# Small linears with both weight parts in one tile, first chunks split by VectorE, row loads later, work reordered at ten places

## What is computed

```python
# block 1: latent attention, 16 heads
c_q, c_kv, k_rope, z = split(x @ w_in, [512, 1024, 1088])
q = rmsnorm(c_q) @ w_qb;  kv = rmsnorm(c_kv) @ w_kvb;  k_rope = rope(k_rope)   # k_rope: 64 columns
x = layernorm(ALPHA*x + (attn(q, k, v) * silu(z)) @ w_out)
# block 2: mLSTM, 8 heads; gates: 16 columns of w_in
qk, v, o, gates, z = split(x @ w_in);  qk = silu(conv4(qk))
x = layernorm(ALPHA*x + (sigmoid(o) * rmsnorm(cell(qk, v, gates)) * silu(z)) @ w_out)
# block 3: mod = silu(c) @ w_ada + b_ada -> sh1, sc1, g1, sh2, sc2, g2
h = rmsnorm(x) * (1 + sc1) + sh1
x += g1 * ((sigmoid(ga) * (attn_a(h) @ w_oa) + sigmoid(gb) * (attn_b(h) @ w_ob)) @ w_out)
h = rmsnorm(x) * (1 + sc2) + sh2
x += g2 * ((silu(h @ w_gate) * (h @ w_up)) @ w_down);  out = rmsnorm(x) * final_w
```

## Time and profile before

| | |
|---|---|
| median of 3 runs | 2233.73 us (2232.44 to 2234.04) |
| profiled execution: its time, its span | 2235.4 us, 2233.7 us |
| TensorE busy, in the span | 2194.4 us (98%) |
| VectorE, ScalarE, GpSimd busy | 1496.7, 1008.7, 265.5 us |
| mean granted TensorE clock | 0.995 of full speed |
| DMA | 500.72 MB, mean 224 GB/s |

### The profile page before, as it was taken

One profiled execution on the slowest core, in us unless ns is written; L12 is line 12 of the kernel. 1 busy time (PEld: TensorE's weight loads), 2 busy tenths in 40 slices (PEclk: granted clock), 3 DMA queues, 4 the chain that ended last, 5 costly groups with the idle time before them and its releaser, 6 DMA issues.

```text
span 2233.7 us, 32562 instructions
## 1 busy us (share of the span) xinstructions
PE 2194.4 (98%) x10958; PEld 1855.2 (83%) x10958; DVE 1496.7 (67%) x2004; ACT 1008.7 (45%) x1229; POOL 265.5 (12%) x499
## 2 busy tenths in 40 slices
PE   9999999999999998999999999999999999999997
PEld 7898878988887777899888888888888888888886
DVE  5766668877666878588776768775565655444544
ACT  5445544544444434434565444454444444443433
POOL 2101110112110010701101111110000100000000
PEclk9999999999999999999999999999999999999999
DMA  8877577679885585968756886766776776565563
GB/s 292 231 192 242 166 255 246 190 224 298 268 270 175 160 302 183 225 219 262 226 180 189 289 279 237 234 218 203 256 228 226 243 247 210 177 221 183 187 200 132
DMA packets 200428, 500.72 MB, mean 224 GB/s; under 512 B 31816, under 2 KB 59112, under 8 KB 200048
## 3 DMA queue, kind: packets, MB, share of 16 engines
q1 hardware_dynamic: 166544, 394.62, 55.1%
q0 software_dynamic: 33760, 104.41, 14.5%
HBM read 496.84 MB, written 2.15 MB: 223 GB/s over the span
## 4 chain that ended last, share of the span: by engine, by line
PE 88%; DVE 6%; ACT 2%; DMA 2%; issue 2%; SPq 0%; DVEq 0%; POOLq 0%; ACTq 0%; POOL 0%
PE ps L2085 74%; PE ps L2123 9%; DVE lo L1149 1%; DMA raw<-in_ml_w_in_dram 1%; ACT hi L660 1%; DVE acc_s L1161 1%; PE ps L2499 1%; PE ps L2489 1%; DMA ada_raw<-in_w_ada_dram 0%; PE ps L2150 0%; DVE conv_tmp L1583 0%; PE ps L2571 0%; PE ps L2161 0%; DMA raw<-in_ml_w_out_dram 0%; PE ps L2414 0%
## 5 line engine op out<-in xcount | busy, mean ns | idle before, releaser
L1149 DVE TENSOR_TENSOR lo<-raw,hi 128x1024 fp32r<-128x1024 f32 x731 | 890.3, 1223 | 573.9 <-ACT hi L660 570.6
L660 ACT CAST hi<-raw 128x1024 fp32r<-128x1024 f32 x731 | 763.2, 1051 | 999.4 <-PE ps L2085 789.0
L2085 PE MATMUL ps<-hi,XH 128*128 128x512 f32 x1944 | 613.4, 395 | 9.0 <-DVE lo L1149 4.7
L2085 PE MATMUL ps<-lo,XH 128*128 128x512 f32 x1944 | 603.3, 390 | 0.0
L2085 PE MATMUL ps<-hi,XL 128*128 128x512 f32 x1944 | 602.4, 390 | 0.0
L2085 PEld LDWEIGHTS ps<-hi,XL 128*128 128x128 f32 x1944 | 365.5, 188 | 77.5
L2085 PEld LDWEIGHTS ps<-lo,XH 128*128 128x128 f32 x1944 | 365.3, 188 | 77.2
L2085 PEld LDWEIGHTS ps<-hi,XH 128*128 128x128 f32 x1944 | 359.7, 188 | 83.4 <-DVE lo L1149 7.5
L578 POOL DMA_DIRECT2D ada_raw<-in_w_ada_dram x384 | 206.2, 537 | 1575.8 <-DVE acc_s L1161 933.1
L1161 DVE SCALAR_TENSOR_TENSOR acc_s<-ada_raw,c_act,acc_s 128x512 f32<-128x512 f32 x256 | 191.0, 746 | 11.7 <-DMA ada_raw<-in_w_ada_dram 10.6
L2123 PE MATMUL ps<-XH,hi 128*128 (+1 forms) x512 | 145.5, 284 | 0.2 <-DVE XL L1300 0.2
(11 more groups left out here) (357 smaller groups left out, 1840.7 us busy)
## 6 DMA issues: line engine op xcount, KB each, us to landing
ada_raw<-in_w_ada_dram POOLq DMA_DIRECT2D x384, 256.0 KB, 4.5
raw<-in_w_in_dram SPq DMA_DIRECT2D x136, 512.0 KB, 4.5
raw<-in_ml_w_in_dram SPq DMA_DIRECT2D x128, 512.0 KB, 4.6
raw<-in_w_gate_dram SPq DMA_DIRECT2D x176, 256.0 KB, 3.0
raw<-in_w_up_dram SPq DMA_DIRECT2D x176, 256.0 KB, 3.6
raw<-in_w_down_dram SPq DMA_DIRECT2D x88, 512.0 KB, 4.2
raw<-in_mla_w_in_dram SPq DMA_DIRECT2D x47, 512.0 KB, 4.5
raw<-in_mla_w_out_dram SPq DMA_DIRECT2D x32, 512.0 KB, 4.7
```

The lines of the kernel that those rows point to most:

```text
L660: nc.scalar.copy(hi[:, j, :], raw[:, j, :]).then_inc(hi_ready, 1)
L1149: nc.vector.tensor_tensor(lo[:, j, :], raw[:, j, :], hi[:, j, :].bitcast(F32), ALU.subtract) \
L2085: ins = mm(ps[:, o:o + HALF], x, w[:, b % RING, c0:c0 + HALF], start=first, stop=(k == n_rows - 1 and x is xl), skip_group_check=True)
```

## The change

It does the following.

- **Small linears:** `small_hi` and `small_lo` become one tile `small_parts`; per 128 rows one matmul of 256 columns takes both parts by XH (128 or 104 weight columns), a second takes the high part by XL. The two partial sums lie in different PSUM partitions. For `kr` they are added by the turn, which multiplies by a table `fold` (two identities on top of each other) instead of an identity; for `gates` VectorE adds them with two more instructions. GpSimd zeroes 1024 instead of 640 columns of `small_raw`, ScalarE casts as many.
- **First chunks:** of `cT` and of `yTa` VectorE makes the high parts of chunks 0 and 1 itself, each followed by its low part; ScalarE starts at chunk 2.
- **First blocks by token half:** the first block of `qr`, `mz1`, `lo0` and `wo0` starts with token half 0 as soon as the reader of that half is done (`first_free`); half 1 waits for the whole reader.
- **yTa** is turned in two halves, the first block of `lo0` between them; the last head's result for the second token half moves behind the first two splits.
- **mlq:** its first block runs all hi x XH, then hi x XL, then lo x XH (`feature_first`), and its `lo_block` stands after the first split.
- **MLA loop:** the second cast of a double slot moves behind `mla_lo` of the next k; ada sums go to the slots without casts (2 less the number of casts).
- **conv:** ScalarE's silu of `mlq` and `mlk` one block later.
- **Row loads** of `lo0` and `lo1`: at blocks 14, 17, 20 and 23 in place of 10, 12, 14 and 16, the tables behind them at 25, 26 and 28.
- **wo0 and ffn0:** the first split of `mTa` before the second product of `ob1`; `lo_block` of ffn0's block 0 before the last rms; both columns of `ada2` in one go before the turn; the second half of `normalise_second` after `modulation`.
- **Tail:** the product of X's first token half by `final_row` moves from VectorE (`last_rows(0)`) to GpSimd, its scaling to ScalarE.

```diff
-        small_hi = at("small_hi", 132, [P, KD, ROPE], F32R)
-        small_lo = at("small_lo", 136, [P, KD, ROPE], F32R)
+        small_parts = at("small_parts", 132, [P, KD, 2, ROPE], F32R)
...
-                if b == 10:
+                if b == 14:
                     sp.wait_ge(tile_split, SPLIT_BASE["yTb"] + 8)
-                if b in (10, 12):
-                    half_row("rows1", row_w, ln_w, 1, (b - 10) // 2)
-                if b in (14, 16):
-                    half_row("rows1", row_b, ln_b, 1, (b - 14) // 2)
-                if b == 18:
+                if b in (14, 17):
+                    half_row("rows1", row_w, ln_w, 1, (b - 14) // 3)
+                if b in (20, 23):
+                    half_row("rows1", row_b, ln_b, 1, (b - 20) // 3)
+                if b == 25:
                     load("window", window[:, :], cst("window"))
-                if b == 22:
+                if b == 26:
                     load("tables2", cos2[:, :, :].rearrange(flat), cst("cos"))
                     load("tables2", sin2[:, :, :].rearrange(flat), cst("sin"))
+                if b == 28:
...
+            pool.wait_ge(ev("final_row"), 16)
+            pool.wait_ge(ev("x_squares"), 9)
+            nc.gpsimd.tensor_tensor(X[:, 0, COLS:], X[:, 0, COLS:], final_row[:, COLS:], ALU.mult) \
+              .then_inc(ev("last_weighted"), 1)
...
-            def mla_casts(slot):
-                for b in MLA_CASTS[slot]:
+            def mla_casts(slot, n0=0, n1=1):
+                for b in MLA_CASTS[slot][n0:n1]:
...
+                if k >= 8:
+                    mla_casts(2 * k - 1 if k == 8 else k + 7, 1, 2)
...
+                    act.wait_ge(ev("last_weighted"), 1)
+                    nc.scalar.mul(X[:, 0, COLS:], X[:, 0, COLS:], ry[:, 0:1]).then_inc(ev("result2"), 1)
...
+                if k < 2:
+                    link(nc.vector.tensor_scalar(CH[:, k, :], ps[:, g + k * SEQ:g + (k + 1) * SEQ], col("q_norm", k),
+                                                 None, ALU.mult))
+                else:
+                    dve.wait_ge(ev("c_hi"), (k | 1) - 1)
                 nc.vector.scalar_tensor_tensor(out=CL[:, k, :], in0=ps[:, g + k * SEQ:g + (k + 1) * SEQ],
...
-            def mla_casts(slot):
-                for b in MLA_CASTS[slot]:
+            def mla_casts(slot, n0=0, n1=1):
+                for b in MLA_CASTS[slot][n0:n1]:
                     lo_block(B_Z0 + b, b % RING)
 
+            mla_sums = [0]
+
             def mla_ada(slot):
-                name, r = ("z0", "mo0")[slot // 16], slot % 16
-                for m in range(ADA_BESIDE[name] * r // 16, ADA_BESIDE[name] * (r + 1) // 16):
-                    ada_block((ADA_FIRST[name] + m) // KD, (ADA_FIRST[name] + m) % KD)
+                for _i in range(2 - len(MLA_CASTS[slot])):
+                    m = ADA_FIRST["z0"] + mla_sums[0]
+                    ada_block(m // KD, m % KD)
+                    mla_sums[0] += 1
 
             for k in range(24):
...
+                if k > 16:
+                    mla_casts(k + 7)
+                if k >= 8:
+                    mla_casts(2 * k - 1 if k == 8 else k + 7, 1, 2)
                 if k < 8:
-                    mla_casts(2 * k)
+                    mla_casts(2 * k, 0, 2)
                 if k < MLA_H:
                     mla_maximum(k)
                 slot = 2 * k + 1 if k < 8 else k + 8
                 if k < 8:
                     mla_ada(slot - 1)
-                mla_casts(slot)
+                if k < 16:
+                    mla_casts(slot)
                 mla_ada(slot)
+            mla_casts(31)
+            assert mla_sums[0] == ADA_BESIDE["z0"] + ADA_BESIDE["mo0"]
 
             def first_residual():
                 dve.wait_ge(ev("x"), 64)
...
-            split_y("yTa", 0, range(8))
+            dve.wait_ge(tiles_turned, BANKS_BEFORE["yTa"] + 1)
+            split_y("yTa", 0, range(2))
+            head_result(7, (1,))
+            split_y("yTa", 0, range(2, 8))
...
                             first3(n0)
+                            split_merged("mTa", 0)
...
+            lo_block(B_FFN, 0)
             rms_token(1, 6, None)
-            normalise_second(2)
-            lo_block(B_FFN, 0)
+            normalise_second((0,))
             modulation("ada2", "norm2", True)
+            normalise_second((1,))
             split_operand(0, "h2_full", B_FFN)
...
                         for tok in range(TOK):
+                            if first_free is not None and b == 0 and tok == 1:
+                                start(name)
                             ins = token_part(g, nb * per_block, H, L, b, tok, per_block, sub)
...
+            def feature_first(n0, g, H, L, need):
+
+                pe.wait_ge(hi_ready, n0 + 1)
+                pe.wait_ge(*need(0))
+                for w, x in ((hi, H), (hi, L), (lo, H)):
+                    if w is lo:
+                        pe.wait_ge(lo_ready, n0 + 1)
+                    for m in range(8):
+                        o = g + m * SEQ
+                        ins = mm(ps[:, o:o + SEQ], w[:, 0, m * P:(m + 1) * P], x[:, 0, :],
+                                 start=w is hi and x is H and m % 2 == 0, stop=False, skip_group_check=True)
+                ins.then_inc(block_done, 1)
+
+            def feature_major(name, n0, nb, H, L, need=None, blocks=None, hi_first=False):
...
                 for k in range(KD):
-                    for w, x in ((small_hi, XH), (small_hi, XL), (small_lo, XH)):
-                        ins = mm(ps[0:n, g:g + SEQ], w[:, k, 0:n], x[:, k, :],
-                                 start=(k == 0 and w is small_hi and x is XH),
-                                 stop=(k == KD - 1 and w is small_lo), skip_group_check=True)
+                    mm(ps[0:ROPE + n, g:g + SEQ], small_parts[:, k, :, :].rearrange(flat)[:, 0:ROPE + n], XH[:, k, :],
+                       start=k == 0, stop=False, skip_group_check=True)
+                    ins = mm(ps[0:n, g:g + SEQ], small_parts[:, k, 0, 0:n], XL[:, k, :], start=False,
+                             stop=k == KD - 1, skip_group_check=True)
                 done(ins)
...
             pe.wait_ge(M2["y"], 8)
-            transposes("yTa", operand_tiles(oz, 0), {8: (M2["h"], 15), 12: (M2["h"], 16)})
             y_tiles = lambda k: (tile_split, SPLIT_BASE["yTa"] + k + 1)
-            token_major("lo0", B_LO, 16, XH, XL, y_tiles, blocks=(0, 6))
+            transposes("yTa", operand_tiles(oz, 0)[:8])
+            token_major("lo0", B_LO, 16, XH, XL, y_tiles, blocks=(0, 1), first_free=(ev("mz1_first"), 1))
+            transposes("yTa", operand_tiles(oz, 0)[8:], {0: (M2["h"], 15), 4: (M2["h"], 16)})
+            token_major("lo0", B_LO, 16, XH, XL, y_tiles, blocks=(1, 6))
             pe.wait_ge(M2["y"], 16)
...
-            ada_columns("ada2", (0, 1), 20,
-                        lambda: (start("h2Ta"), turn_first("h2Ta", h_norm, h2_ready, first_token)))
-            turn_first("h2Ta", h_norm, h2_ready, second_token)
+            ada_columns("ada2", (0, 1), 20)
+            start("h2Ta")
+            turn_first("h2Ta", h_norm, h2_ready, [(k, t) for k in range(8) for t in range(TOK)])
```

More of the change, by code:

```diff
@@ L701, in each_tok @@
                         ins = nc.scalar.copy(dst(tok), src(T(name, tok, width)))
+                    if tok == 0 and first is not None:
+                        ins.then_inc(first, 1)
                 ins.then_inc(freed_sem["act"], 1)
@@ L790, in _ @@
             first3(B_QR)
-            each_tok("z1", lambda t: z_tok[:, t, COLS:], ACT.Silu)
+            each_tok("z1", lambda t: z_tok[:, t, COLS:], ACT.Silu, first=ev("z1_first"))
             g = grp("cT")
-            for k in range(8):
+            for k in range(2, 8):
                 if k % 2 == 0:
@@ L1752, in rms_token, with normalise_second @@
                 rsqrt(1, 1.0 / D, src, ev("rms"), at=tok)
-            def normalise_second(n):
-                for half in range(n):
+            def normalise_second(halves):
+                for half in halves:
                     cols_ = slice(half * COLS, (half + 1) * COLS)
@@ L2052, in _ @@
             last_quarter(0)
-            last_rows(0)
             last_quarter(1)
@@ L2367, in _ @@
             x1_tiles = chunks_ready("x1Ta")
-            feature_major("mlq", B_CONV, 16, XH, XL, x1_tiles, blocks=(0, 5))
+            feature_major("mlq", B_CONV, 16, XH, XL, x1_tiles, blocks=(0, 5), hi_first=True)
             pe.wait_ge(ev("normed0"), 2)
```

139 lines of the change are left out of this document (77 added, 62 removed).

## The result

| | before | after |
|---|---|---|
| median | 2233.73 us (2232.44 to 2234.33, 5 runs) | 2221.01 us (2219.88 to 2223.01, 5 runs) |
| profiled execution: time, span | 2235.4, 2233.7 us | 2221.0, 2219.3 us |
| TensorE's last matmul ends; from there to the end | 2221.4; 12.3 us | 2206.6; 12.7 us |

The ratio is 0.9945 (95% interval 0.9934 to 0.9955): 12.7 us less between the medians, 14.4 between the two profiled executions. The forecast was 2219.3.

What follows compares the result with a forecast made beforehand. TensorE was taken as the bound, busy 2194.4 of 2233.7 us. Terms summed to 14.4 us: 2235.4 to 2221.0 profiled, less 1.7 gives a median of 2219.3; range 2215.0 to 2226.0, the forecast's own 2217 to 2222.

Steps and rivals of the forecast that it cites:

- Small linears: Both small linears: 16 matmuls at 0.1135 and 16 at 0.120 us replace 48 in each; 3.4 us less.
- cT, mz1, wo0, ffn0: TensorE's waits at these places shrink or close: cT 1.6 us, mz1 0.7, wo0 and ffn0 together 1.8.
- MLA: Latent attention loop: ada sums leave both two-cast rounds, shortening waits for YL; 1.4 us, bounds 0.5 and 2.3.
- mlq and conv: mlq's first block and the convolution's later silu: no wait over 0.3 us found; 0, bound 0.8 upward.
- yTa: Turn yTa: waits of 0.34 and 1.10 us can vanish, limited by VectorE's 0.59 us slack; 0.5, between 0 and 0.9.
- VectorE was the bound: Rival: gains at MLA, yTa, wo0 and ffn0 are worth nothing, TensorE waits later; 2223.0 us, chance 0.12.
- Row loads: lo0 and lo1: later row loads free queued weight loads; wait 3.83 plus clock 1.7, together 5.5, less 0.5: 5.0 us.
- Tail: End of kernel: VectorE's product moves to GpSimd; between 1.2 us better and 0.6 worse, taken as 0.
- the tail is blocked: Rival: VectorE's short operations stand still while GpSimd multiplies, losing half a microsecond; 2219.9 us, chance 0.15.
- h_norm: TensorE's 4.1 us wait for h_norm from ScalarE: said to stay, with no term in the sum.

Runs made afterwards that it cites:

- mla_sums_old: Changed kernel with one ada sum per slot of the latent attention's loop, as before the change; TensorE's lead drops by 1.3 us in all.
- x1_old: Changed kernel with mlq's first block in the old order; TensorE loses 0.5 us from the turn x1Ta to the first chunks.
- rows_old: Changed kernel with the row loads back at blocks 10, 12, 14 and 16 of lo0, tables at 18 and 22; median 2224.15 us.
- ctl: The changed kernel run once more, with no edit; median 2220.90 us, profiled execution 2222.64 us.
- tail_gap: Changed kernel with the product by final_row on VectorE, to acc_g, while VectorE waits for ScalarE's squares; median 2218.95 us.

## Why the prediction held, and where it didn't

The sum for the profiled execution, 2221.0, was hit, partly by errors that cancel: 2.8 us of gain that I had not seen, against 0.8 less than forecast at yTa, 1.2 lost behind `h_norm`, 0.4 in the tail and 0.3 in the first blocks, where the profiles of the changed kernel and its variants lie up to 0.5 apart themselves. That the sum came out to the tenth is luck; that most of its terms did is not.

- **Small linears** (3.4): 3.6. Right in size and mechanism.
- **cT, mz1, wo0, ffn0** (1.6, 0.7, 1.8): 1.8, 0.9, 1.6. Right; each wait went where the rows said, though no run takes these edits back.
- **MLA** (1.4): 1.35, and mla_sums_old shows that it hangs on the two sums. The way there was another than forecast: both waits for YL closed altogether (the lead rises by 2.5 us, the better bound and more), and 1.1 came back in the next rounds, as a wait of 0.36 us for the probabilities at 273.86 and one of 0.61 for YL at 277.72.
- **mlq and conv** (0): 2.8. I had looked for waits of TensorE only. 0.3 of it is a shorter wait ahead of x1Ta, 0.5 the new first block and 0.9 the low clock of 3.41 us, which is no wait in any list (half its length would be 1.7, but x1_old waits 0.6 us longer for the split at full clock). Whether the low stretch stays away for good, or was one execution's, one profile of before can't tell. Of the 1.1 in the convolution at most 0.4 are the silu.
- **yTa** (0.5): -0.3. The step that failed is "0.5, between 0 and 0.9": the slack that I counted lay behind the split, but VectorE's own two high parts, 0.96 us of new work, were not in the sum. Nor did both waits vanish: of 0.34 and 1.10 us one of 0.75 is left. The rival "VectorE was the bound" held here, but not at wo0 and ffn0; in the MLA loop 1.1 of 2.5 came back.
- **Row loads** (5.0): 4.6, by rows_old 4.3. Right: 5.5 were expected of the hole alone, and the lead rose by 5.7. The 0.5 that was taken off for row loads amid weight loads was too small: 1.1 were lost here, at a DMA share of 1.01 in a part of the stretch, and a wait of up to 1.5 us more comes in some executions.
- **Tail** (0): -0.4. The rival "the tail is blocked" is what happened, near its price of half a microsecond. My upper price for GpSimd's product, 2.6 us, was nearer than the MEMSET's 1.04: it takes 2.36. The Trainium skill ("SBUF — State Buffer", section "SBUF: two separate sides") is borne out to 0.02 us: the VectorE operation with two SBUF inputs ends when GpSimd's does, and the ones with a single input run on. The estimate of 2.25 us from the Trainium skill's "GPSIMD Engine Reference", section 3.1, compares with 2.36 and 2.40 measured.
- **h_norm** (0): -1.2. The forecast left this wait as it was, and it is: 4.05 us in both. Behind it the clock falls, and what that costs depends on when; this term was not in the sum.

**From the profile to the median** is the step by which the forecast missed 1.7 us. I took the 1.7 between the profiled execution of before and its median as a constant and subtracted it again. After the change the profiled execution (2221.0) lay on the median (2221.01), and the one of ctl 1.7 above it. A profiled execution is one draw from the spread. The one of before, 2235.4, lay above its five other runs (2232.44 to 2234.33), but in other sessions the same kernel reached 2236.05.

The low clock behind `h_norm`, by windows of the changed kernel and then of tail_gap (PE busy first after the length, clock third from the end):

```profile
857.00:859.00 2.00, 0.22 (x2) 0.22 (x3) 1.69 (x11) 1.75 (x4) 0.00 (x0) 1.00 0.00 0
859.00:861.00 2.00, 1.80 (x13) 1.57 (x12) 1.93 (x4) 1.95 (x3) 0.00 (x0) 0.70 0.00 0
861.00:863.00 2.00, 1.69 (x7) 1.22 (x6) 1.62 (x6) 1.82 (x5) 0.00 (x0) 0.50 0.39 68
...
865.00:867.00 2.00, 2.00 (x7) 1.57 (x6) 1.97 (x4) 1.02 (x2) 0.00 (x0) 0.59 0.83 250
```

```profile
861.00:863.00 2.00, 2.00 (x12) 2.00 (x11) 1.96 (x3) 1.79 (x3) 0.00 (x0) 0.51 0.00 0
863.00:865.00 2.00, 1.69 (x9) 1.23 (x8) 1.46 (x6) 1.89 (x4) 0.00 (x0) 0.64 0.34 59
865.00:867.00 2.00, 2.00 (x10) 1.65 (x9) 1.97 (x3) 1.02 (x2) 0.00 (x0) 1.00 0.52 203
```

The same wait of 4.05 us was followed by a low stretch of 6.83 us in eight profiles (with the one of before, nine) and of 3.41 in five, starting 2.0 to 5.4 us after the wait began. In before it started at 871.3, 2.1 us behind the start of the wait, and so 1.9 of its 6.83 us fell on a TensorE that stood; in the changed kernel it started 5.1 behind it and fell on work. By estimate that is half of 1.9, 1.0 of the 1.2. In rows_old the stretch was 3.41 us long, and so of 4.3 us for the move (and 0.8 lost before it) 3.2 are left in the profile, and 3.1 between the medians. What decides between the two lengths isn't shown.

## What to carry to other kernels

- Price an edit by the chain of the engine that TensorE will wait for next, with the new work that the edit gives it. A wait that is closed ahead of a full chain reappears at the chain's next meeting point.
- An instruction that waits for a DMA holds everything behind it on its engine. The weight's low part was late three times here because an optional sum stood ahead of it.
- Don't give GpSimd a product on SBUF while VectorE's operations with two SBUF operands are on the critical path; a gap of VectorE's own took the same product for nothing.
- Before a difference is put down to an edit, look at how the same stretch varies in kernels that don't have the edit: the convolution's 0.4 us didn't pass that.
